# All modulation passes behind the read of weighted values, gating a step later, scores that wait for the queries alone

## What is computed

```python
for l in range(2):                       # layer
    shift, scale, gate = silu(c) @ ada_w[l] + ada_b[l]      # modulation, also for c_ctx
    h = rmsnorm(x) * (1 + scale) + shift
    qA, kA, vA, qB, kB, vB, qC, kC, vC, g = split_cols(h @ w_in[l])
    yA = global attention, 8 heads, 2 of keys, q and k normalised and roped
    yB = neighbourhood attention, 8 heads, with a bias by position
    yC = window attention, 8 heads, 2 of keys, roped, with a sink
    x = x + gate * (concat(yA, yB, yC) * silu(g)) @ w_out[l]
```

## Time and profile before

| | |
|---|---|
| median of 3 runs | 2989.78 us (2987.14 to 2992.57) |
| the profiled execution | 2997.7 us, span 2995.9 |
| mean granted clock of TensorE | 0.985 of full |
| TensorE busy | 2842.1 us, 95% of the span |
| VectorE busy | 1345.9 us, 45% |
| ScalarE busy | 757.6 us, 25% |
| GpSimd busy | 186.4 us, 6% |

### The profile page before, as it was taken

The page is one execution under the profiler, slowest core; times in us unless marked ns, Lnnn a source line. Parts: engine busy times, 40 slices in busy tenths (PEclk is TensorE's granted clock), DMA queues, the critical chain, the costliest instruction groups (busy, mean ns, idle before and its releaser), DMA issues.

```text
span 2995.9 us, 33583 instructions
## 1 busy us (share of the span) xinstructions
PE 2842.1 (95%) x13144; PEld 1501.5 (50%) x13144; DVE 1345.9 (45%) x2544; ACT 757.6 (25%) x1375; POOL 186.4 (6%) x225
## 2 busy tenths in 40 slices
PE   7988899999999999999999999999999998999998
PEld 3555555655555656567544544444443434444442
DVE  2785776675346565574475841111213523121112
ACT  3233454441222354332261120000002122000001
POOL 1322212100001100000000000000000000000000
PEclk9999999999999999999999999999999999999999
DMA  7343323111145433102111048999993216999996
GB/s 287 96 144 130 104 70 99 57 71 57 56 148 168 153 120 120 43 29 113 47 59 39 28 187 341 421 421 421 421 421 156 79 76 270 410 421 422 421 420 285
DMA packets 90670, 586.56 MB, mean 196 GB/s; under 512 B 10192, under 2 KB 10192, under 8 KB 29232
## 3 DMA queue, kind: packets, MB, share of 16 engines
q1 hardware_dynamic: 69696, 502.56, 41.7%
q0 software_dynamic: 20848, 82.26, 8.4%
HBM read 582.68 MB, written 2.10 MB: 195 GB/s over the span
## 4 chain that ended last, share of the span: by engine, by line
PE 68%; DVE 6%; ACT 2%; DMA 1%; issue 1%; DVEq 0%; ACTq 0%
PE BIG L1046 44%; PE PJ L1046 10%; PE BIG L1839 4%; PE PT L1375 2%; PE PT L1391 1%; PE PT L1046 1%; PE BIG L1358 1%; DMA W<-in_mod_rows 1%; PE PJ L1095 1%; PE BIG L1362 1%; PE PT L1815 1%; ACT ARENA L2043 0%; DVE ARENA L2882 0%; PE BIG L1351 0%; DVE ARENA L2881 0%
## 5 line engine op out<-in xcount | busy, mean ns | idle before, releaser
L1046 PE MATMUL BIG<-ARENA 128*64 128x512 f32 (+3 forms) x2608 | 540.8, 462 | 4.8 <-DVE ARENA L2904 2.5
L1046 PEld LDWEIGHTS BIG<-ARENA 128*64 128x64 f32 (+1 forms) x2608 | 282.1, 168 | 250.0 <-issue 224.2
L1046 PE MATMUL PJ<-HT,W 128*128 128x512 f32 (+2 forms) x1040 | 400.1, 533 | 7.3 <-DVE ARENA L2573 2.6
L1046 PE MATMUL BIG<-HT,W 128*128 128x512 f32 (+1 forms) x768 | 320.9, 579 | 2.4 <-DVE ARENA L2739 2.1
L1046 PE MATMUL BIG<-W,ARENA 128*64 128x512 f32 (+1 forms) x1280 | 282.0, 573 | 0.9 <-DVE ARENA L2785 0.9
L1046 PEld LDWEIGHTS PJ<-HT,W 128*128 128x128 f32 x1040 | 193.8, 193 | 164.6 <-issue 125.4
L2933 DVE SCALAR_TENSOR_TENSOR XC<-BIG,MOD,XC 128x512 f32<-128x512 f32 x128 | 90.2, 747 | 379.7 <-PE BIG L1839 379.7
L2054 ACT ACTIVATE ARENA<-PT 128x512 f32<-128x512 f32 (+1 forms) x264 | 145.5, 583 | 448.8 <-PE PT L1375 448.4
L2341 DVE CUSTOM_DVE_ANT_0 SPILL<-W,VEC 128x1024 bf16<-128x1024 f32 x168 | 228.2, 1359 | 62.4 <-DMA W<-in_mod_rows 54.9
L1046 PEld LDWEIGHTS BIG<-HT,W 128*128 128x128 f32 x768 | 146.8, 192 | 173.3 <-issue 165.8
L1375 PE MATMUL PT<-CONST,ARENA 128*128 128x128 f32 x1024 | 155.6, 288 | 39.4 <-DVE ARENA L2492 30.8
(11 more groups left out here) (302 smaller groups left out, 2901.8 us busy)
## 6 DMA issues: line engine op xcount, KB each, us to landing
ARENA<-in_exp_w SPq DMA_DIRECT2D x168, 1024.0 KB, 18.3
W<-in_exp_w SPq DMA_DIRECT2D x144, 1024.0 KB, 16.8
W<-in_units SPq DMA_DIRECT2D x89, 1024.0 KB, 4.9
HT<-in_exp_w SPq DMA_DIRECT2D x72, 1024.0 KB, 22.1
W<-in_mod_rows POOLq DMA_DIRECT2D x128, 512.0 KB, 3.9
ARENA<-in_bias_b POOLq DMA_DIRECT2D x16, 384.0 KB, 4.4
XC<-in_x SPq DMA_DIRECT2D x1, 3072.0 KB, 11.9
XC<-in_x POOLq DMA_DIRECT2D x1, 3072.0 KB, 12.0
```

Of the source, the lines that this page charges most:

```text
L1046: ins = pe.matmul(out, lhsT, rhs, start=start, stop=stop, skip_group_check=skip)
```

## The change

1. `schedule` puts all passes of a step behind `O`, the read of weighted values; `with_modulation` is gone. In the order they now stand directly ahead of `S` of the step after next.
2. `MODS_ROOM` of layer 1 becomes 2.6 for B pairs (3.2 before) and 2.6 for A pairs (1.8).
3. In layer 0, `gate` of a B pair (not the first) goes one step later than its `tanh`.
4. In layer 1, C pairs with j over 0 rope their queries ahead of the gates' products.
5. In layer 1, `q_ready` and `k_ready` of B pairs are set by queries and keys alone. Before, each later product (values, gates) overwrote `q_ready`, so that the first scores of a pair waited for the gates' eviction.
6. In layer 0, ScalarE no longer preloads the table of Tanh behind `norm_q`.
7. Variables named `use` get names of their own in norms and ropes.

```diff
-MODS_ROOM = [{"B": 3.6, "A": 1.4, "C": 0.0}, {"B": 3.2, "A": 1.8, "C": 0.0}]
+MODS_ROOM = [{"B": 3.6, "A": 1.4, "C": 0.0}, {"B": 2.6, "A": 2.6, "C": 0.0}]
...
-        return out + by_blocks(i, "qg", 1) + [("tanh", i), ("gate", i)]
+        return out + by_blocks(i, "qg", 1) + [("tanh", i)] + ([("next", i)] if i else []) + [("gate", i)]
...
-        return out + gates[:KT] + [("rope_q", i)] + gates[KT:] if parts == 2 else out + gates + [("rope_q", i)]
+        return out + [("rope_q", i)] + gates
...
-def with_modulation(todo, mods):
...
             mods = [("mod", x) for x in range(len(MOD_OPS)) if mod_step(x) == at]
-            early = 1 if layer == 0 and steps[n][0] < 4 else 2
-            order += mods[:early]
-            mods = mods[early:]
...
-        if n >= 0:
-            order += with_modulation(todo, mods)
-        else:
-            order += todo
+        order += todo
...
             order.append(("O", n))
+            order += mods
...
-                            if PAIRS[i][0] == "B":
+                            if PAIRS[i][0] == "B" and which in ("k", "q"):
                                 (k_ready if which == "k" else q_ready)[i] = ("use", use)
...
-                        if what == "norm_q":
+                        if what == "norm_q" and layer:
                             act.preload_act_table(ACT.Tanh)
```

More of the change, by code:

```diff
@@ L1301, in attention @@
                             if b > a:
-                                use = next_pj()
-                                pe.matmul(PJ[use[0]][:, 0:b - a], const("blk"), SQT[:, a:b],
+                                bank = next_pj()[0]
+                                pe.matmul(PJ[bank][:, 0:b - a], const("blk"), SQT[:, a:b],
                                           start=True, stop=True).then_inc(pj_filled, 1)
@@ L1311, in attention @@
                         src = K[:, kv % 2, 0:N] if what == "rope_k" else Q[:, x % 2, 0:N]
-                        use = next_pj()
-                        pe.matmul(PJ[use[0]][:, 0:N], const("rot"), src, start=True, stop=True)\
+                        bank = next_pj()[0]
+                        pe.matmul(PJ[bank][:, 0:N], const("rot"), src, start=True, stop=True)\
                             .then_inc(pj_filled, 1)
@@ L2020, in attention @@
                             if b > a:
-                                use = me.next_pj()
-                                act.wait_ge(pj_filled, use[2])
-                                act.activation(SQT[:, a:b], PJ[use[0]][:, 0:b - a], ACT.Ln,
+                                norm_use = me.next_pj()
+                                act.wait_ge(pj_filled, norm_use[2])
+                                act.activation(SQT[:, a:b], PJ[norm_use[0]][:, 0:b - a], ACT.Ln,
                                                bias=EPSC[:, bias:bias + 1], scale=scale)\
-                                    .then_inc(pj_free[use[0]], 1)
-                        act.wait_ge(pj_free[use[0]], use[1] + 1)
+                                    .then_inc(pj_free[norm_use[0]], 1)
+                        act.wait_ge(pj_free[norm_use[0]], norm_use[1] + 1)
                         act.activation(SQT[:, 0:n], SQT[:, 0:n], ACT.Exp, scale=-0.5).then_inc(qk_rs, 1)
-                        if what == "norm_q":
+                        if what == "norm_q" and layer:
                             act.preload_act_table(ACT.Tanh)
@@ L2457, in attention @@
                         dst = K[:, kv % 2, 0:N] if what == "rope_k" else Q[:, x % 2, 0:N]
-                        use = me.next_pj()
-                        dve.wait_ge(pj_filled, use[2])
+                        rot = me.next_pj()
+                        dve.wait_ge(pj_filled, rot[2])
                         roped = me.next("qk_roped") - 1
@@ L2462, in attention @@
                             dve.wait_ge(qk_roped, roped)
-                        dve.tensor_tensor(ROPE_T, PJ[use[0]][:, 0:N], const("sin"), ALU.mult)\
-                            .then_inc(pj_free[use[0]], 1)
+                        dve.tensor_tensor(ROPE_T, PJ[rot[0]][:, 0:N], const("sin"), ALU.mult)\
+                            .then_inc(pj_free[rot[0]], 1)
                         link(dve.tensor_tensor(dst, dst, const("cos"), ALU.mult))
-                        dve.wait_ge(pj_free[use[0]], use[1] + 1)
+                        dve.wait_ge(pj_free[rot[0]], rot[1] + 1)
                         dve.tensor_tensor(dst, dst, ROPE_T, ALU.add).then_inc(qk_roped, 1)
```

## The result

The changed kernel takes 3060.8 us (median of 4 runs, 3057.3 to 3065.0), the one before 2989.1 in the same comparison: ratio 1.024, interval 1.022 to 1.026, so it is 71.7 us slower. The forecast was 3028, 38 us slower, range 2975 to 3055: the direction held, the size was about half, and the time lies 6 us above the range. The profiled executions are nearer to each other: 3058.5 and 2997.7 us, spans 3056.7 and 2995.9, 60.8 us apart. The remaining 11 us are the place of these single executions among the runs: that of the kernel before took 8.6 us more than its median, that of the changed kernel 2.3 us less.

A forecast was written before the change was run, and what follows sets the result against it. TensorE, busy in 95% of the span, bounds the kernel through its waits. Terms 26 + 5 + 1 + 8 + 7 - 3.6 = +43 us, less 5 for clock: 2989.8 + 38 = 3028 us, range 2975 to 3055.

The forecast's parts named there:

- All three waits: TensorE's waits to be removed: transposes for the read 30.8 us, layer 1's scores for gates 9.7, C pairs' roping 3.6.
- the rival that they would move to the transposes: Layer 1: transposes behind the scores wait for the same VectorE queue, 9.7 us becomes 4; +5, no chance given.
- The passes ahead of the maxima: Layer 0's B steps: 2, 3, 4 passes make maxima 2.1, 3.5, 4.85 us late; stalls are delay less tolerance, sum 51.7.
- 5.95 us in step 7 and 4.5 in steps 4 and 10: Layer 0's B pairs: TensorE's predicted stall in each of these steps, delay of the maxima less the step's tolerance.
- the term of step 14: Layer 0's B pairs: predicted stall 5.3 us, with 3 us more because the step's weight rows are single.
- The clock: Granted clock given back where waits go: 5 us in layer 0, about 7 and 1.7 in layer 1's B and A pairs.
- Pair 4: Layer 0, pair 4 projected: batches ahead of maxima, normalisation and roping add +2.0, +5.8, +0.7, +2.2 us.
- The +1 for its first 12 steps: Layer 1's B pairs: new stalls 17 us, removed 9.7 and about 7 of clock, so +1.
- +5, +5: Layer 1's A pairs: two batches of 3 in a row make VectorE's step 14 us, stalling TensorE +5 and +5.
- The rival "row loads": Layer 0: batches wait for rows as in layer 1, 3 us more in some 10 steps, 3055 us or more; chance 0.12.
- Gating "costs nothing either way": Layer 0's B pairs: VectorE does the gating product once anyway, so moving it a step later costs nothing.
- The rule on GpSimd and VectorE: Two-input VectorE passes contend with GpSimd reading SBUF; moved away from its adds, each gets 0.6 to 0.9 us cheaper.

The follow-up runs named there:

- run 2: The changed kernel with the passes and their room put back where they were before, its other parts kept: 2981.0 us, ratio 0.997.
- run 1: The kernel before with only the placement changed, all passes of a step behind its read of weighted values: 3088.3 us, ratio 1.032.
- run 4: The changed kernel with each step's passes one item later, behind the maxima of the next scores: 3019.7 us, ratio 1.009.
- run 3: As run 2, with the gating of B pairs back in its old step: 2976.4 us, ratio 0.996.
- run 9: As run 3, with the last pass of each step behind the read and the others ahead of it: 2958.6 us, ratio 0.989.
- run 10: As run 9, but with the last two passes of each step behind the read: 2979.2 us, ratio 0.997.
- run 12: As run 9, with room 3.2 and 2.0 in layer 0, 3.0 and 1.8 in layer 1: 2954.5 us, ratio 0.988.
- run 6: The changed kernel with only the first two row tiles of modulation weights loaded and all passes made on them: 3018.7 us, ratio 1.010.
- run 5: The changed kernel with each modulation pass over 512 of its 1024 columns, loads unchanged: 3010.3 us, ratio 1.006.

## Where the prediction held, and the step that failed

**What bounds the kernel, and what is removed: right.** All three waits went, by the rows above. Layer 1's scores and the C pairs' roping gave 11 and 3.9 us in run 2, where nothing was added in layer 1. Of the rival that they would move to the transposes (9.7 becoming 4) run 2 shows 2.3 us, the changed kernel 0.4.

**The passes ahead of the maxima: right, step by step.** Run 1 puts the loss there, run 4 wins 41 us by one item, runs 3, 9 and 10 show the tolerance: one pass below it, two above. The forecast's 51.7 us of standing in layer 0's B steps is 47.3 by the window. Three of its largest terms, 5.95 us in step 7 and 4.5 in steps 4 and 10, come out at 5.1, 5.2 and 5.2. (By the text's own rule the term of step 14 is 4.85 + 3 - 2.2 = 5.65 and not 5.3; the sum moves by 0.3.)

**The clock: the step that failed, in sign.** The prediction gave the clock back wherever it removed a wait ("I take 5 off for the clock in layer 0", "about 7 of clock" and "about 1.7 of clock" in layer 1), 13.7 us in all, and charged none for the stalls it added, although show the low clock in a stretch that holds a stall. So its sum of 38 is about 52 of standing less 14 of clock. Measured are 41.9 of standing and 18.9 more of busy time. The clock terms are wrong by 33 us, more than the 23 by which the sum falls short of the profiled 60.8; the standing was 10 too high and hid the rest.

TensorE's busy time for the same matmuls, with the mean granted clock:

| kernel | clock | TensorE busy us | median us |
|---|---|---|---|
| run 12 | 0.991 | 2826.4 | 2954.5 |
| run 9 | 0.990 | 2830.0 | 2958.6 |
| before | 0.985 | 2842.1 | 2988 to 2990 |
| run 4 | 0.980 | 2850.9 | 3019.7 |
| run 6 | 0.980 | 2854.4 | 3018.7 |
| after | 0.976 | 2861.0 | 3060.8 |
| run 1 | 0.972 | 2870.4 | 3088.3 |

The two go together in every kernel here. With two levels of the clock, 1.2 and 2.4 GHz, a mean of 0.985 over 2996 us is 90 us at the lower one, 0.976 over 3057 us is 147. In a stretch right behind the stall that ends at 150.45 the column of the clock reads:
```profile
150.00:160.00 10.00, 9.55 (x40) 5.67 (x41) 4.61 (x9) 1.93 (x3) 2.68 (x3) 0.75 0.06 12
```
0.75 is half of those 10 us at each level. Before it TensorE had stood for 5.2 us. No run held TensorE busy through its stalls, so the clock's part is read from busy time and not shown by an experiment of its own.

**Pair 4: mis-sized.** In its six steps I took +10.7 and it is +21.8. By the waits TensorE stands 20.0 us there: 6.0 at VectorE's eviction (I had 5.8 more than the old 0.9), 5.4 at roping, 5.2 and 2.5 at the normalisation; it stood 5.2 before. So standing grew by 14.8, since normalisation and roping wait longer than my 2.0 and 2.2, and busy time by 7.1, at a clock of 0.87 instead of 1.00. The waits of these six steps:
```profile
PE PJ L1019 <- DVE ARENA L2412: 6.0, 1, 6.0
PE PJ L1019 <- DVE ARENA L2436: 5.4, 1, 5.4
PE PJ L1276 <- ACT ARENA L1962: 5.2, 1, 5.2
PE PJ L1276 <- ACT ARENA L2048: 2.5, 1, 2.5
```
**Layer 1: two errors that cancel in the B pairs.** The +1 for its first 12 steps against the measured +0.2 is luck. The 7 us of clock did not come back (0.97 before and after), and the standing was over-priced: a batch of 3 was taken at 9.1 us from one pass that began at 898.77, 6.2 us after its load was issued at 892.62, while the page of the profile before has
```profile
W<-in_mod_rows POOLq DMA_DIRECT2D x128, 512.0 KB, 3.9
```
as the median from issue to landing, and the batch shown above took 6.7. In the A pairs the standing was right: scores wait 6.7 us for roping in two places that waited 1.8 before, where the forecast had "+5, +5". The +10.9 instead of +7 is the clock, +3.2 where 1.7 was to come back.

**Row loads: priced.** In layer 0's B steps I had 11 us. There VectorE waits 11.9 us for rows, and run 6 shows 13.5 for the stage. The rival "row loads" gave 3055 or more, which is nearest to the measured time, but not by its mechanism: it had 3 us more in some 10 of layer 0's steps, the rows are late in 6 places there, and 30 us stay without any load.

**Gating "costs nothing either way": open.** In its new place VectorE makes it 1.18 us long instead of 1.80 (mean, beside GpSimd's adds there). It stands ahead of a read that is late already: at the first place that moved, TensorE waits 4.3 us for that read in run 2 and 1.7 in run 3, while a wait for an eviction a step earlier is 0.4 in run 2 and 2.2 in run 3. Net it costs 0.9 us of standing in layer 0's B steps; the other 3 us of the stage are the clock's, which scatters by as much (run 3).

**The rule on GpSimd and VectorE.** Passes moved away from GpSimd's adds are shorter:
```profile
L2314 DVE CUSTOM_DVE_ANT_0 SPILL<-W,VEC 128x1024 bf16<-128x1024 f32 x56 | 72.4, 1292 | 15.0 <-DMA W<-in_mod_rows 11.9 <-issue 0.2
```
1292 ns for 1413 in the earlier trace rows, 6.7 us less over 56 passes. The Trainium skill (SBUF — State Buffer, Who interferes with whom) has two SBUF inputs contend with a reading GpSimd; the trace agrees. The sum had clean passes already, so this moves nothing in it. The rescaling of context tiles, moved beside the adds in turn, went from 0.35 to 1.1 us, and in the step shown that one stands on the path.

**Open.** The medians are 71.7 us apart, the profiled executions 60.8. The timed executions of the changed kernel have clocks of 0.973 to 0.976, those of the kernel before, in the later comparisons, mostly 0.986 or 0.987, so part of these 11 us may be the clock again. That is not shown. The Tanh preload left out in layer 0 had no run of its own; in run 2, which leaves it out, pair 4's six steps take 67.1 us, as before.

## What to carry to other kernels

Work that fills gaps on an in-order engine has two neighbours: what it delays and what it lets through. Measure the slack of both in the trace (here 0.7 to 3.4 us for the maxima, as counted in the prediction) and give each side no more than fits; one pass behind the read and the others ahead of it beat all on one side. Price a new stall at more than its length, because the clock was lower behind it and the matmuls that followed took longer: 18.9 us on 41.9 of standing here. That is no fixed rate; with half passes (run 5) it was 9.3 us on 3.3. Where removed waits are credited with clock, added ones have to be charged with it. And a batch that needs more operands than it has buffers is longer than its passes; take the length of a load from its median and not from one row.

## What the runs showed of the hardware

Across the seven kernels of the table, with the same 13144 matmuls, TensorE's busy time spans 2826 to 2870 us and follows the mean granted clock from 0.991 to 0.972: 44 us that no matmul in the program explains.

The same 2.46 us of standing in the same step went with a fall of the clock in one execution (0.87 over the step, 10.74 us busy for 62 matmuls) and not in another (1.00, 9.25 us).

A rescaling of 128x256 values on VectorE, which has one tensor input, took 0.35 us alone and 1.05 to 1.10 beside GpSimd's adds; an eviction of 128x384 from PSUM beside them stayed at 0.55.
